# Two units instead of three run token tile by token tile at the seams of the projections

## The reference, cut to what matters

```python
def first_block(x, ...):
    ...
    x = x + mix @ w_out                      # 1024 x 1024
    h = rms_norm(x, norm2_w)
    gate, val = split(h @ ffn_w_up)          # 1024 x 6144
    x = x + (gelu(conv(gate)) * val) @ ffn_w_down   # 3072 x 1024
    return rms_norm(x, norm_f_w)

def second_block(x, ...):                    # two layers
    for l in range(2):
        h = (silu(h1 @ w_gate) * (h1 @ w_up)) @ w_down      # h1 = rmsnorm(x, g[0])
        x = x + 0.5 * rmsnorm(h, g[1])
        h = hybrid_mixer(rmsnorm(x, g[2]), ...)             # ends in "@ w_out", 1024 x 1024
        x = x + rmsnorm(h, g[3])
        h = (silu(h3 @ w_gate) * (h3 @ w_up)) @ w_down      # h3 = rmsnorm(x, g[4])
        x = x + 0.5 * rmsnorm(h, g[5])
    return x
```

## Time and profile before

| what | value |
| --- | --- |
| median of 3 runs | 1447.44 us (1444.27, 1447.44, 1447.52) |
| the profiled execution's own time | 1445.5 us |
| its span in the trace | 1443.4 us |
| granted TensorE clock over the span | 0.998 |
| DVE busy, ACT busy | 966.8 us (67%), 741.9 us (51%) |
| weights and inputs read | 256.69 MB |

### The profile page before, as it was taken

The page is one execution under the profiler, slowest core; times in us unless marked ns, Lnnn a source line. Parts: engine busy times, 40 slices in busy tenths (PEclk is TensorE's granted clock), DMA queues, the critical chain, the costliest instruction groups (busy, mean ns, idle before and its releaser), DMA issues. The chain is left out here.

```text
span 1443.4 us, 21346 instructions
## 1 busy us (share of the span) xinstructions
PE 1421.9 (99%) x8866; PEld 1249.7 (87%) x8866; DVE 966.8 (67%) x1169; ACT 741.9 (51%) x955; POOL 129.2 (9%) x124
## 2 busy tenths in 40 slices
PE   7999999999999999999999999999999999999998
PEld 7899999999988888888988888888888898888886
DVE  5967886688864766546977656556665579666644
ACT  6535763555643644446656444454444467554442
POOL 4001000100000100001721000010000145100000
PEclk9999999999999999999999999999999999999999
DMA  7736465766655667456325755547754462466542
GB/s 247 253 123 199 147 220 176 188 192 179 197 183 171 219 205 232 146 195 156 125 98 174 218 176 189 190 147 250 230 188 166 146 174 103 147 195 197 177 162 101
DMA packets 251828, 259.13 MB, mean 180 GB/s; under 512 B 26691, under 2 KB 213716, under 8 KB 251732
## 3 DMA queue, kind: packets, MB, share of 16 engines
q1 hardware_dynamic: 250704, 255.49, 56.1%
q10 hardware_dynamic: 1028, 2.28, 0.5%
HBM read 256.69 MB, written 1.05 MB: 179 GB/s over the span
## 5 line engine op out<-in xcount | busy, mean ns | idle before, releaser
L1140 DVE TENSOR_TENSOR w_lo<-raw,w_hi 128x2048 fp32r<-128x2048 f32 (+1 forms) x240 | 540.3, 2254 | 309.9 <-ACT w_hi L698 309.6
L698 ACT ACTIVATE w_hi<-raw 128x2048 fp32r<-128x2048 f32 (+1 forms) x238 | 452.0, 1901 | 313.8 <-PE psm L1859 153.3
L1859 PE MATMUL stream<-w_hi,a_pair 128*128 128x512 f32 (+1 forms) x1152 | 361.3, 386 | 3.2 <-DVE a_pair L1179 2.8
L1859 PE MATMUL stream<-a_pair,w_hi 128*128 128x256 f32 x2016 | 357.1, 280 | 0.6 <-DVE w_lo L1140 0.3
L1859 PEld LDWEIGHTS stream<-a_pair,w_hi 128*128 128x128 f32 x2016 | 307.1, 188 | 2.2 <-DVE w_lo L1140 0.5
L1859 PE MATMUL stream<-a_pair,w_lo 128*128 128x256 f32 x1008 | 281.0, 279 | 0.0
L1859 PEld LDWEIGHTS stream<-w_hi,a_pair 128*128 128x128 f32 x1152 | 214.1, 188 | 48.2 <-issue 2.7
L1859 PE MATMUL stream<-w_lo,a_pair 128*128 128x512 f32 (+1 forms) x576 | 220.7, 383 | 0.0
L1859 PEld LDWEIGHTS stream<-a_pair,w_lo 128*128 128x128 f32 x1008 | 189.7, 188 | 0.0
L1859 PE MATMUL psm<-w_hi,h_hi 128*128 128x512 f32 x448 | 175.1, 391 | 0.0
L1859 PE MATMUL psm<-w_hi,h_lo 128*128 128x512 f32 x448 | 174.4, 389 | 0.0
(11 more groups left out here) (291 smaller groups left out, 1470.2 us busy)
## 6 DMA issues: line engine op xcount, KB each, us to landing
raw<-in_ffn_w_up SPq DMA_DIRECT2D x136, 512.0 KB, 5.1
raw<-in_ffn_w_down SPq DMA_DIRECT2D x104, 512.0 KB, 4.5
raw<-in_ffn_w_gate SPq DMA_DIRECT2D x88, 512.0 KB, 4.0
raw<-in_w_in SPq DMA_DIRECT2D x80, 512.0 KB, 4.8
raw<-in_w_out SPq DMA_DIRECT2D x24, 512.0 KB, 4.2
raw<-in_w_ret_o SPq DMA_DIRECT2D x8, 512.0 KB, 4.3
raw<-in_w_lru_o SPq DMA_DIRECT2D x8, 512.0 KB, 4.5
diag<-in_conv_diag SPq DMA_DIRECT2D x8, 512.0 KB, 5.7
```

Source lines behind the costliest of these rows:

```text
L698: nc.scalar.activation(w_hi[s][:, :, 0:n], raw[s][:, :, 0:n], ACT.Copy).then_inc(w_hi_ready, 1)
L1140: return V.tensor_tensor(w_lo[s][:, ks, 0:n], raw[s][:, ks, 0:n], w_hi[s][:, ks, 0:n].bitcast(F32), ALU.subtract)
L1859: return nc.tensor.matmul(dst, lhs, rhs, start=start, stop=stop, skip_group_check=True)
```

## The change

One constant changes, and with it the one place where the number was written out.

```diff
-HELD = 3
+HELD = 2
@@ ffn(c0, f, i, next_turn)
-                    if (j, t) == (2, 0):
+                    if (j, t) == (HELD - 1, 0):
                         second_tile()
```

## The result

| | before | after |
|---|---|---|
| median, us (lowest to highest, runs) | 1447.48 (1444.27 to 1447.58, 4) | 1456.28 (1454.38 to 1457.8, 4) |
| ratio, after to before | | 1.0071, 95% interval 1.005 to 1.0091 |
| the profiled execution, us (span) | 1445.5 (1443.4) | 1454.38 (1452.3) |
| mean granted clock of TensorE | 0.998 | 0.994 |

A forecast was written before the change was run, and what follows sets the result against it. PE bounds the kernel, so its new waits add: seam 1 1.0, seam 2 1.95, seams 3 and 6 0.25 each, 4 and 7 1.95 each, 5 1.35, 8 0: 8.7 us on the 1447.44 median gives 1456 us, range 1451.5 to 1461.

The forecast's parts named there:

- PE sets the end, and every wait adds to the time: Whole kernel: PE is busy 1421.9 of 1443.4 us, so every microsecond it newly waits is added to the time.
- The head: Turn of tile 1, seams 2, 4, 5, 7: PE arrives before x_t; +1.92 us at 4 and 7, +1.30 at 5, +1.31 at 2.
- The tail: Turn of tile 0, one pass (2.72 us) after c11/0: waits 0.65 us at seam 2, 0.3 at seam 1, 0.05 to 0.15 elsewhere.
- shift of tile 1's `x_t`: Seam 2, head: the later subtraction of c12 delays tile 1's x_t by 0.2 us (0 to 0.6).
- a later `lo(c14)` runs beside less of POOL's work: Seam 2: less contention with POOL gives part of the delay back; without it the sum would be 0.3 us higher.
- Seams 1, 3 and 6: Added time of 1.0 us at seam 1 and 0.25 us each at seams 3 and 6.
- shift of a subtraction to behind the turn: Seam 1: half subtraction of c12 falls behind tile 0's turn, moving tile 1's second addition 0.7 us (0 to 1.1).
- margin of 0.36 us at seam 3: Seam 3, turn of tile 1: x_t's first half was ready 0.36 us early; a shift of about 0.4 uses that up.
- The clock: Rival at the heads' new waits: granted clock falls, 1.5 us each; two falls give 1459 us, four 1462; chance 0.25.
- a granted clock of 0.5 behind the waits: Sign of being wrong: the profile after shows the granted clock at 0.5 behind PE's new waits.
- The cover came back: Rival at the four heads: tile 1's x_t comes with the passes, PE finds it ready; 1445.8 us; chance 0.05.
- nothing of the head's cost was hidden: Rival: ACT and DVE fall back only by half, heads cost 3.2 us instead of 6.5; 1451 to 1452 us; chance 0.12.

The follow-up runs named there:

- heads alone: Against the kernel before, two held units at the heads only, the tails hold three: 1454.15 us, ratio 1.0051.
- late split: Against the changed kernel, ACT rounds and DVE subtracts c14 behind tile 1's new x_t at seams 2, 4, 5 and 7: 1448.41 us.
- one unit: Against the changed kernel, HELD = 1 in place of 2: 1494.95 us, ratio 1.0342 to the kernel before.
- tails alone: Against the kernel before, two held units at the tails only, the heads run three on tile 0: 1448.89 us, ratio 1.0008.
- the heads alone with the late split: Against the kernel before, HEAD = 2 with HELD = 3, and c14's split behind tile 1's new x_t: 1446.56 us, ratio 0.9992.

## Why the prediction was right, and where a term was off

*PE sets the end, and every wait adds to the time.* Right: seam by seam the added waits and the added time agree.

*The head.* Right in mechanism and size. A wait of 2.35 us was read ahead for seam 4; the weight load waited 2.50 and the matmul 2.08. The distances from the turn of tile 0 to `lo(c14)` and to `x_t` held to 0.01 us. The four heads were worked out as 1.92 + 1.92 + 1.30 + 1.31; seams 4 and 5 alone, in the kernel with the heads alone, gave 2.05 and 1.36. That the order on ACT and DVE is the cause was argued; the kernel with the late split shows it.

*The tail.* At seams 4, 5 and 7 it is nothing, as worked out. At seam 2 the matmul waited 0.50 and the weight load 0.92, around the 0.65 of the prediction, and the 1.97 us of that seam fit the 1.95. The shift of tile 1's `x_t` was 0.13 us (477.05 - 466.93 = 10.12 behind the turn, before 9.99), where 0.2 was taken. The reason that the prediction gave for it, that a later `lo(c14)` runs beside less of POOL's work, did not come true. Here it is after the change:

```profile
473.45 2.87 DVE L1140 TENSOR_TENSOR w_lo<-raw,w_hi 128x2048 fp32r<-128x2048 f32 x1
```

It took 2.87 us against 2.82 before, and POOL's half of c13 covers its first 0.72 us against 0.66. That POOL is what makes it long is borne out: at all four heads of before and after it takes 2.8 us or more with POOL's row over its start, and 2.28 in its later place, where POOL subtracts nothing. DVE's own half of c13, which begins together with POOL's, is not slowed (1.23 us, elsewhere 1.22).

*Seams 1, 3 and 6* were set too high: 0.7 for 1.0, 0.1 for 0.25 each. The term that failed there is the shift of a subtraction to behind the turn. The margin of 0.36 us at seam 3 was not used up. Together this makes 0.5 us of the 8.7.

*The clock.* The forecast gave the rival a chance of 0.25 and left it out of the sum. It also named a granted clock of 0.5 behind the waits as a sign of being wrong, and that sign came at two of the four heads: two falls in each of two profiles of the changed kernel, 1.4 and 1.6 us in the first of them, close to the 1.5 worked out from the earlier trace rows. The Trainium skill, "TensorE: Matmul & The Clock Gate", the section on why this matters, warns of idle gaps between matmul bursts from a certain length on. The runs agree for the longest waits (eleven falls at eleven, with one unit), and for those of 1.4 to 2.6 us they show both (five falls at twelve). So the cause of the time is the forecast's, 8.2 us, and one rival's on top, 3.0: 11.2 us by the trace.

*The number.* 1456.0 was forecast and 1456.28 measured, and that is closer than the steps are; in part it is luck. The spans differ by 8.9 us, not 11.2, since this execution happened to have a start that was slower by 3.3 us and a stage that was faster by 5.1, neither of which the change touches (the mixers make up the rest, -0.4). The medians differ by 8.8 here and by 8.57 in the run of the same kernel beside the later experiments. Both are below the 11.2: over many executions the falls are probably fewer than two, which the mean clocks of 0.994 to 0.997 allow but don't show, since only profiled executions can be read seam by seam.

*The other rivals.* The cover came back in no part (the distances held), and nothing of the head's cost was hidden.

## What to carry to other kernels

When PE's order is shortened by a pass at a hand-over, ask whether the engines that feed it still have the order that was made for the longer one: here the same instructions in PE's new order cost 8.8 us, and moving one weight split behind the other tile's chain took all but 1.0 us of it away. Measure cover from the event that starts the chain to the moment that PE asks for its result: the third pass was worth 8.8 us, the second four times as much. And read an effect of 1 or 2 us from a distance inside the trace, since a total of this kernel moves by 5 us for reasons that have nothing to do with the edit.

## What the runs showed of the hardware that was not expected

The first block's up projection, a stage of 256-column matmuls, runs at one of two spacings, for the whole stage, from one execution to the next. The window from 275 to 400 us, first of before and then of after, both at a granted clock of 1.00:

```profile
275.00:400.00 125.00, 125.00 (x1063) 125.00 (x1063) 102.65 (x152) 72.39 (x110) 0.00 (x0) 1.00 0.70 194
```

```profile
275.00:400.00 125.00, 125.00 (x1105) 125.00 (x1105) 106.55 (x155) 75.99 (x113) 0.00 (x0) 1.00 0.70 196
```

PE had no idle time in either, and did 1105 matmuls in place of 1063: 113.3 against 117.8 ns apart in the timelines, 5.1 us over the stage. Of the ten profiles, four had the short spacing (after, the tails alone, the heads alone, and the heads alone with the late split) and six the long one (before and the same changed kernel run again among them), so it goes with no edit. An earlier stretch of 256-column matmuls has the same two spacings and chooses for itself: there before and the tails alone have the short one, up to about 195 us, and the other eight the long one. The window from 178 to 188 us, of before and then of after:

```profile
178.00:188.00 10.00, 10.00 (x91) 10.00 (x90) 6.88 (x5) 6.70 (x6) 0.00 (x0) 1.00 0.56 181
```

```profile
178.00:188.00 10.00, 10.00 (x87) 10.00 (x86) 8.98 (x7) 5.43 (x6) 0.00 (x0) 1.00 0.57 192
```

The times of before fall into two groups as well, most between 1446 and 1449 us, some between 1441 and 1443.5, with two between the groups. The profiled executions of the four kernels with the short spacing in the up projection are the shortest or second shortest of their kernels' runs. What chooses between the two is open.
